# One loop over all turns of a layer's experts, and the overflow part moved behind it

## The chip, the cores and the metric

The kernel runs on one core of a Trainium2 chip. The metric is the device time of one execution in microseconds (us). The kernel before took 1077.97 us, the median of three runs (1076.32, 1077.97 and 1079.43).

## The reference

The program is a two-layer decoder trunk over 256 tokens of width 1024, all in float32. Each layer has a token mixer (a spatial gate with attention in layer 0, a short convolution in layer 1) and then a mixture of 32 experts; the mixture is what the change touches:

```
expert_idx = top_g[:, None] * EXPERTS_PER_GROUP + top_e        # 1 of 4 groups, then 2 of its 8 experts
combine = jnp.sum(one_hot(expert_idx, 32) * weights[..., None], axis=1)
for e in range(N_EXPERTS):                                     # 32
    h = jax.nn.silu(t @ w_gate[e]) * (t @ w_up[e])             # (256,1024) @ (1024,512), twice
    out = out + combine[:, e:e + 1] * (h @ w_down[e])          # (256,512) @ (512,1024)
```

An expert's three matrices are 2 MB each, 6 MB together; two layers of 32 experts read 402 MB of the run's 440 MB.

## The kernel before

The kernel is written engine by engine: each engine has its own program, and semaphores are all that ties them. For each expert up to 32 tokens (CAP) are gathered; a token list longer than that is finished in the overflow part.

For expert e TensorE (PE) does, in this order: gate and up for its 32 gathered tokens (`gate_up`, L1579, 64 float32 matmuls, which the trace shows as 128 matmuls and 128 weight loads of two passes); the scatter of expert e-1's result into the PSUM banks 0 to 3, where the layer's output is summed (`scatter`, L1596); two transposes (L1602); the gather of expert e+1's tokens (L1608); and down (L1588). VectorE (DVE) builds the selection matrices and the product of gate and up; ScalarE (ACT) does silu and copies out of PSUM. SyncE (SP) issues the weight loads into a ring of nine 2 MB slots, that is three experts. Experts 0 to 11 and the last two (30, 31) are loaded matrix by matrix, experts 12 to 29 with one 6 MB transfer each (`whole`, L433), issued once the down of the expert three before has been done (`y_ready`).

The experts are worked on in turns of three (TRI = 3, TURNS = 10, so turns 0 to 9 hold experts 0 to 29). Turn 0 is written out. Then PE has three loops with a body of three experts each: turns 1 to 3 (`apart_expert`, with a wait for each matrix), turn 4 alone (`whole_expert`, one wait), and, after the overflow part, turns 5 to 9 (MIDDLE = 5). SP, ACT and DVE also go through the turns in two loops with the overflow part between them. The last two experts are written out behind the last loop (`last_experts`).

The overflow part stands after expert 14 (PAUSE = MIDDLE*TRI - 1). On PE it begins with `put_x` (L1354), which adds the residual x to the PSUM sums with eight matmuls (16 in the trace). Then each of the four engines reads the number of overflow blocks from memory into a register (`further`, L357) and branches over a body that would scatter the last result and process the blocks, one after the other (`more_experts`, and `overflow` on SP). At 0 blocks the branch is taken and nothing of the body runs.

An engine's instructions come from memory too: the profile's queue q8 carries PE's instruction stream.

Of the kernel before, what the change touches and what calls it, by code (L numbers as in the profile page):

```python
# [23 lines left out]
NE = G * EG  # L24
# [10 lines left out]
RING = 9  # L35
LAG = 2
SLOT = 4096
TRI = 3
# [7 lines left out]
L_EVEN = 0  # L46
EARLY = 2
RING_FIRST = (0, 1, 3)
MIDDLE = 5
PAUSE = MIDDLE * TRI - 1  # L50
SPARE_XG = 1
PER_MOE = 3 * NE - 3
L_MOE = [7, 7 + PER_MOE + 9]
# [13 lines left out]
def entry(l, e):  # L67
    return L_MOE[l] + 3 * (e - (e > EARLY))


def place(n):
    return (n + 2) % RING
# [3 lines left out]
    return place(L_MOE[l] + 3 * i) // 3  # L76


def is_whole(e):
    return FINE <= e < NE - 2  # L80


SINGLE = [z for z in SPLIT if z not in (L_EVEN, L_EVEN + 1, L_ODD)]
for layer in range(2):
    for expert in range(FINE):
        if expert != EARLY:
            SINGLE += [entry(layer, expert) + mat for mat in range(3)]
    SINGLE += [entry(layer, NE - 2) + mat for mat in range(3)]
    SINGLE += [entry(layer, NE - 1) + mat for mat in range(2)]
SINGLE.append(L_GAIN)  # L90
WHOLE = [(layer, expert) for layer in range(2) for expert in range(NE) if is_whole(expert)]


def single_count(n):
    return sum(z <= n and place(z) == place(n) for z in SINGLE)


def whole_count(l, e):
    return sum((zl, ze) <= (l, e) and place(entry(zl, ze)) == place(entry(l, e)) for zl, ze in WHOLE)


def pieces(n):
# [20 lines left out]
def trunk(nc, x_in, even_first, even_second, even_w_in, even_w_out, gmlp_w_s, gmlp_b_s, columns,  # L123
          odd_first, odd_w_in, odd_w_out, norm_gains, router, expert_weights_in, last_down, norm_final, out):
    with ExitStack() as ctx:
# [3 lines left out]
        def sem(name):  # L129
            return ctx.enter_context(nc.semaphore(name))  # L130
# [112 lines left out]


        landed = [sem(f"landed{i}") for i in range(RING)]
        whole_landed = [sem(f"whole_landed{i}") for i in range(RING // 3)]
        gate_used, out_half = sem("gate_used"), sem("out_half")
        first_landed = [sem(f"first_landed{i}") for i in range(len(OPENING))]
        eps_ready = sem("eps_ready")
# [60 lines left out]
        def wide(n):  # L310
            return slot(n).rearrange("p (k f) -> p k f", k=K)

        def tall(n):
            return slot(n).rearrange("p (j d) -> p j d", j=4)
# [33 lines left out]

        def wait_landed(eng, n):

            eng.wait_ge(landed[place(n)], 16 * single_count(n))

        @contextmanager
        def further(eng):
# [24 lines left out]
        def _(sp):  # L379
# [49 lines left out]
            def whole(l, e, i, former):  # L429

                at = third(l, (i - 1) % TRI)
                sp.wait_ge(y_ready, after(l, former))
                sp.dma_start(ring[:, SLOT * 3 * at:SLOT * 3 * (at + 1)], expert_weights_in[l, e]).then_inc(whole_landed[at], 16)  # L433

            def turns(l, start, stop):
                with sp.Fori(start, stop) as b:
                    for i in range(TRI):
                        whole(l, b * TRI + i, i, b * TRI + (i - TRI))
# [16 lines left out]
            def experts(l):  # L455
                if l:
                    first(l, 2, 2)
                    load_spare(l)
                first(l, 0, 0)
                first(l, 0, 1)  # L460
                if l == 0:
                    load_spare(l)
                first(l, 0, 2)
                first(l, 1, 0)
                if l == 0:
                    first(l, 1, 1)
                sp.wait_ge(*((even_lo, 6), (pb_ready, 4))[l])
                load_early(l, 0, 0, 1)
                first(l, 1, 2 - l)
                first(l, 2, 1 - l)  # L470
                load_early(l, 1, 0, 2)
                first(l, 1 + (l == 0), 2 * l)
                first(l, 2, 2 - l)
                load_early(l, 1, 1, 2)
                for e in range(EARLY + 2, FINE):
                    second(l, e)
                for i in range(TRI):
                    e = FINE + i
                    whole(l, e, i, e - TRI)
                turns(l, ROLLED + 1, MIDDLE + 1)  # L480
                overflow(l)
                turns(l, MIDDLE + 1, TURNS)
                for e in LAST_TWO:
                    for mat in range(2):
                        n = entry(l, e) + mat
                        fill(n, matrix(l, e, mat), buffer(n, mat))
                n = entry(l, NE - 2) + 2
                fill(n, matrix(l, NE - 2, 2), tall(n))
                n = entry(l, NE - 1)
                sp.wait_ge(*used_up(n + 2 - RING))  # L490
                for j in range(NP):
                    sp.dma_start(tall(n + 2)[:, j, :], last_down[l, j]).then_inc(quarter_landed[j], 16)
# [76 lines left out]
        def _(act):  # L569
# [197 lines left out]
            def expert(l, e):  # L767
                act.wait_ge(gu_ready, after(l, e))
                act.activation(sg, GU[:, 0:FP], ACT.Silu).then_inc(silu_ready, 1)  # L769
                act.wait_ge(cmb_turned, after(l, e))  # L770
                act.activation(cmb, BB[:, 0:S], ACT.Copy).then_inc(cmb_ready, 1)  # L771
                act.wait_ge(y_ready, after(l, e))
                act.activation(yy, YB[:, 0:DP], ACT.Copy).then_inc(yy_ready, 1)  # L773
# [11 lines left out]
            def moe(l):  # L785

                act.wait_ge(tops_ready, l + 1)
                for t in range(TT):
                    act.activation(gs[:, t, :], lg[:, t, :], ACT.Exp, bias=gneg[:, t:t + 1], scale=rstd[:, t:t + 1],
                                   accum_out=gsum[:, t:t + 1])  # L790
                    last = act.activation(ex[:, t, :], ml[:, t, 0:NE], ACT.Exp, bias=eneg[:, t:t + 1],
                                          scale=rstd[:, t:t + 1])
                last.then_inc(exps_ready, 1)
                preload(ACT.Silu)
                for start, stop in ((0, MIDDLE), (MIDDLE, TURNS)):
                    with act.Fori(start, stop) as b:
                        for i in range(TRI):
                            expert(l, b * TRI + i)
                    if start == 0:
                        more_experts(l)  # L800
                last_experts(l)

            def more_experts(l):
# [42 lines left out]
        def _(dve):  # L846
# [400 lines left out]
            def moe(l):  # L1247

                update(l)
                for t in range(TT):  # L1250
                    copy_turned(l, t)
                invert(l, 1)
                fillers()
                route(l)
                choose(0, count[:, 1:CAP + 1], 0).then_inc(sel_ready, 1)
                gather(l, 0, 0)
                expert_weights(l)
                over_capacity(l)
                weigh(l, 0).then_inc(wsel_ready, 1)
                for i in range(TRI):  # L1260
                    expert(l, 0, i)
                    if i == 0:
                        more_blocks(l)
                for start, stop in ((1, MIDDLE), (MIDDLE, TURNS)):
                    with dve.Fori(start, stop) as b:
                        for i in range(TRI):
                            expert(l, b, i)
                    if start == 1:
                        more_experts(l)
                for e in range(TURNS * TRI, NE):  # L1270
                    expert(l, e // TRI, e % TRI, last=e == NE - 1)

# [53 lines left out]
        def _(pe):  # L1326
# [328 lines left out]

                expert(l, EARLY, EARLY, wait_weights, lambda mat: lambda k: halves[mat][k // HK][:, k % HK, :], spare)

            def apart_expert(l, T, i):
                n = entry(l, TRI + i)

                def wait_weights(mat):
                    pe.wait_ge(landed[place(n + mat)], (T + (single_count(n + mat) - 1)) * 16)

                expert(l, T * TRI + i, i, wait_weights, lambda mat: lambda k: wide(n + mat)[:, k, :], tall(n + 2))

            def whole_expert(l, T, i):
                n = entry(l, FINE + i)

                def wait_weights(mat):
                    if mat == 0:  # L1670
                        pe.wait_ge(whole_landed[place(n) // 3], (T + (whole_count(l, FINE + i) - ROLLED)) * 16)

                expert(l, T * TRI + i, i, wait_weights, lambda mat: lambda k: wide(n + mat)[:, k, :], tall(n + 2))

# [15 lines left out]
            def moe(l):  # L1690
# [26 lines left out]
                for e in range(TRI):  # L1717
                    if e == EARLY:
                        early_expert(l)
                    else:  # L1720
                        first_expert(l, e)
                with pe.Fori(1, ROLLED) as T:
                    for i in range(TRI):
                        apart_expert(l, T, i)
                with pe.Fori(ROLLED, MIDDLE) as T:
                    for i in range(TRI):
                        whole_expert(l, T, i)
                for t in range(TT):
                    put_x(t)
                more_experts(l)  # L1730
                with pe.Fori(MIDDLE, TURNS) as T:
                    for i in range(TRI):
                        whole_expert(l, T, i)
                last_experts(l)
                scatter_result(l, NE - 1).then_inc(o_ready, 1)

# [83 lines left out]
```

## Time and profile before

| what | value |
|---|---|
| median of three runs | 1077.97 us |
| span of the profiled execution | 1076.0 us |
| PE busy, weight loads busy | 820.6 us (76%), 653.4 us (61%) |
| DVE, ACT, POOL busy | 315.3, 192.6, 5.4 us |
| memory traffic | 439.94 MB, mean 409 GB/s |
| instructions on PE | 13956 matmuls, 13957 weight loads |

The profile was taken from one execution. Its own time is its span, 1076.0 us; it is 1.97 us below the median of the three runs. A wait named `<-DMA` is one for weights. `<-issue` is time in which an engine waited for nothing that the profile shows. Layer 0's experts run from about 113 to 537 us of the span, the odd layer's mixer from 542 to 634 us, and layer 1's experts from 643 to 1067 us. Expert 12 of layer 0 begins its gate at 255.54 us, expert 15 behind the overflow part at 302.92 us, expert 29 at 505.42 us and expert 30 at 514.40 us; in layer 1 the same experts begin at 786.10, 832.26, 1035.31 and 1045.56 us.

### The profile page before, as it was taken

What the parts mean: (1) busy time and instruction counts of PE and PEld (TensorE: products, weight loads), DVE (VectorE), ACT (ScalarE), POOL (GpSimd) and SP (SyncE); (2) the same over time, 40 slices, a digit from 0 to 9 for tenths busy, and PEclk for the clock granted to TensorE, in tenths of its full rate; (3) what the DMA queues carried; (4) which work ended last, traced back from release to release, by engine and by line L of the source; (5) the groups of instructions that cost most, each with busy time, mean ns of one, the idle gap of its engine ahead of it and who ended that gap; (6) DMA issues with size and microseconds to landing.
All of it is one profiled execution on the core that took longest, in us unless ns stands there. A gap on an engine that the chain in (4) does not pass through costs nothing.

```text
span 1076.0 us, 30244 instructions
## 1 busy us (share of the span) xinstructions
PE 820.6 (76%) x13956; PEld 653.4 (61%) x13957; DVE 315.3 (29%) x782; ACT 192.6 (18%) x360; POOL 5.4 (1%) x26
## 2 busy tenths in 40 slices
PE   9999989673767667666899999896556767666685
PEld 9778757452654545555599977664354545555463
DVE  5764522211111111111277744221101111111112
ACT  6764211000000000000254331010000000000002
POOL 1000000000000000000000000000000000000000
PEclk9999999987887888888999999998879888888889
DMA  9987999999999999999998599999999999999995
GB/s 375 427 332 282 422 427 427 429 441 425 433 427 434 433 432 431 433 433 421 418 428 336 219 396 424 426 427 429 444 425 428 432 432 433 429 435 433 433 420 242
DMA packets 24948, 439.94 MB, mean 409 GB/s; under 512 B 2992, under 2 KB 3504, under 8 KB 8240
## 3 DMA queue, kind: packets, MB, share of 16 engines
q1 hardware_dynamic: 23904, 437.58, 95.9%
q10 hardware_dynamic: 976, 1.33, 0.4%
q8 instruction: 58, 0.95, 0.4%
q14 instruction: 10, 0.08, 0.0%
HBM read 437.84 MB, written 1.05 MB: 408 GB/s over the span
## 4 chain that ended last, share of the span: by engine, by line
DMA 53%; PE 40%; issue 4%; DVE 2%; SPq 1%; ACT 1%; DVEq 0%; ACTq 0%
DMA ring<-in_expert_weights 50%; PE psum L1579 12%; PE psum L1375 6%; PE psum L1588 6%; PE psum L1448 4%; PE psum L1596 3%; PE psum L1608 3%; PE psum L1427 2%; DMA ring<-in_even_w_in 2%; DMA m<-in_gmlp_w_s 1%; PE psum L1602 1%; PE psum L1700 1%; DVE ring_halves L875 0%; PE psum L1347 0%; PE psum L1334 0%
## 5 line engine op out<-in xcount | busy, mean ns | idle before, releaser
L1579 PE MATMUL psum<-ring,m 128*32 128x128 f32 x7936 | 304.1, 322 | 221.5 <-DMA ring<-in_expert_weights 187.2
L1579 PEld LDWEIGHTS psum<-ring,m 128*32 128x32 f32 x7936 | 280.7, 132 | 252.5 <-issue 177.9
L1236 DVE TENSOR_TENSOR m<-psum,m 128x128 f32<-128x128 f32 x64 | 18.7, 292 | 549.3 <-ACT m L769 532.4
L1588 PE MATMUL psum<-ring,m 128*32 128x256 f32 x1984 | 123.3, 387 | 5.2 <-DMA ring<-in_expert_weights 3.9
L769 ACT ACTIVATE m<-psum 128x128 f32<-128x128 f32 x60 | 16.7, 278 | 497.1 <-PE psum L1579 497.1
L1375 PE MATMUL psum<-scr_halves,ring_halves 128*128 128x256 f32 x736 | 99.1, 284 | 0.2 <-ACT ring_halves L603 0.2
L1588 PEld LDWEIGHTS psum<-ring,m 128*32 128x32 f32 x1984 | 66.1, 113 | 52.9 <-issue 12.1
L1375 PEld LDWEIGHTS psum<-scr_halves,ring_halves 128*128 128x128 f32 x736 | 94.3, 193 | 0.5 <-ACT ring_halves L603 0.5
L1596 PE MATMUL psum<-m 32*128 32x256 f32 x1024 | 81.1, 420 | 10.6 <-issue 8.5
L1608 PE MATMUL psum<-x,m 128*32 128x256 f32 x1024 | 72.7, 402 | 1.4 <-issue 0.8
L1596 PEld LDWEIGHTS psum<-m 32*128 32x128 f32 x1024 | 50.2, 195 | 29.6 <-issue 23.6
L875 DVE TENSOR_TENSOR ring_halves<-ring,ring_halves 128x2048 fp32r<-128x2048 f32 (+1 forms) x32 | 63.6, 2021 | 12.4 <-ACT ring_halves L603 12.4
L603 ACT ACTIVATE ring_halves<-ring 128x2048 fp32r<-128x2048 f32 (+2 forms) x40 | 57.8, 1477 | 31.7 <-PE psum L1375 24.4
L1210 DVE STREAM_TRANSPOSE m<-psum 128x256 f32<-128x256 f32 x64 | 28.8, 450 | 105.4 <-PE psum L1608 105.4
L773 ACT ACTIVATE m<-psum 128x256 f32<-128x256 f32 x60 | 23.0, 384 | 157.7 <-PE psum L1588 157.7
L1608 PEld LDWEIGHTS psum<-x,m 128*32 128x32 f32 x1024 | 27.6, 112 | 25.0 <-issue 13.8
L1219 DVE TENSOR_SCALAR m<-count,pos,cw 128x128 f32<-128x128 f32 x128 | 38.2, 341 | 0.1
L771 ACT ACTIVATE m<-psum 128x256 f32<-128x256 f32 x60 | 23.0, 384 | 83.5 <-PE psum L1602 83.4
L1448 PE MATMUL psum<-ring_halves,aux_halves 128*128 128x512 f32 x96 | 33.2, 400 | 0.0
L1205 DVE TENSOR_SCALAR m<-count,pos,rstd 128x32 f32<-128x32 f32 x128 | 32.1, 294 | 2.1 <-issue 1.8
L1602 PE MATMUL psum<-ident,m 128*128 128x128 f32 x128 | 28.8, 307 | 0.0
L1213 DVE TENSOR_TENSOR m<-m,gains 128x256 f32<-128x256 f32 x64 | 27.2, 425 | 2.2
(196 smaller groups left out, 522.5 us busy)
## 6 DMA issues: line engine op xcount, KB each, us to landing
ring<-in_expert_weights SPq DMA_DIRECT2D x36, 6144.0 KB, 33.7
ring<-in_expert_weights SPq DMA_DIRECT2D x76, 2048.0 KB, 21.9
ring<-in_odd_w_in SPq DMA_DIRECT2D x5, 2048.0 KB, 26.0
ring<-in_even_w_in SPq DMA_DIRECT2D x3, 2048.0 KB, 22.2
ring<-in_even_w_out SPq DMA_DIRECT2D x2, 2048.0 KB, 31.4
spare<-in_expert_weights SPq DMA_DIRECT2D x2, 2048.0 KB, 24.7
ring<-in_last_down SPq DMA_DIRECT2D x8, 512.0 KB, 32.1
ring<-in_odd_w_out SPq DMA_DIRECT2D x2, 2048.0 KB, 28.9
```

The source lines that it names most:

```text
L603: act.activation(hi_slot(n)[:, c], raw_part(n, part), ACT.Copy).then_inc(w_hi, 1)
L875: dve.tensor_tensor(lo_slot(n)[:, c], raw_part(n, part), hi_slot(n)[:, c].bitcast(F32), ALU.subtract).then_inc(w_lo, 1)
L1205: last = dve.tensor_scalar(sel[:, t, CAP * i:CAP * (i + 1)], ranks, pos[:, bass.ds(at(e, t), 1)], rstd[:, t:t + 1], ALU.is_equal, ALU.mult)
L1210: return dve.transpose(xg[:, i, :, :], XB[:, 0:DP].rearrange("p (q k) -> p k q", k=K))
L1219: last = dve.tensor_scalar(wsel[:, t, :].rearrange("p (n c) -> p n c", n=NP), count[:, 1:CAP + 1].unsqueeze(1).to_broadcast([P, NP, CAP]), ...
L1375: return pe.matmul(bank[banks[c // 2]][:, (c % 2) * S:(c % 2 + 1) * S], w[a][:, k, P * c:P * (c + 1)], h[b][:, k, :], start=k == 0 and a + ...
L1448: last = pe.matmul(bank[2 * t + c][:, :], mix[a][:, 4 * r + j, P * t:P * (t + 1)], w[b][:, j, 512 * c:512 * (c + 1)], start=r == 0 and j = ...
L1579: last = pe.matmul(GU[CAP * part:CAP * (part + 1), lo:lo + FP], block_of(k), w_of(k)[:, FP * part:FP * (part + 1)], start=k == 0, stop=k = ...
L1588: last = pe.matmul(YB[CAP * part:CAP * (part + 1), 0:DP], h[:, CAP * f:CAP * (f + 1)], w[:, f, DP * part:DP * (part + 1)], start=f == 0, s ...
L1596: last = pe.matmul(bank[part][:, DP * t:DP * (t + 1)], cmb[r, P * t:P * (t + 1)], yy[r, :], start=first and t == 0, stop=False, skip_group ...
L1602: last = pe.transpose(BB[:, P * t:P * (t + 1)], wsel[:, t, :], ident[:, :])
L1608: last = pe.matmul(XB[CAP * part:CAP * (part + 1), 0:DP], sel[:, t, CAP * i:CAP * (i + 1)], x[:, t, DP * part:DP * (part + 1)], start=t == ...
```

## The change

PE, ACT and DVE go through all turns of a layer in one loop; SP has one loop for the loads of experts 15 to 29. The overflow part with `put_x` stands behind the loop, that is after expert 29 and before the last two (PAUSE = 29). On PE the bodies of turn 4 and of turns 5 to 9 are gone, since one body now serves turns 1 to 9. To make that possible all experts count on the same semaphores: a whole 6 MB load increments the first slot's semaphore when it lands, and SP increments the other two right after it has issued the load, so that the body's waits for matrices 1 and 2 are met. A whole expert so has two more waits on PE than before.

```diff
-MIDDLE = 5
-PAUSE = MIDDLE * TRI - 1
+PAUSE = TURNS * TRI - 1
...
-                sp.dma_start(ring[:, SLOT * 3 * at:SLOT * 3 * (at + 1)], expert_weights_in[l, e]).then_inc(whole_landed[at], 16)
+                sp.dma_start(ring[:, SLOT * 3 * at:SLOT * 3 * (at + 1)], expert_weights_in[l, e]).then_inc(landed[3 * at], 16)
+
+                sp.sem_inc(landed[3 * at + 1], 16)
+                sp.sem_inc(landed[3 * at + 2], 16)
...
-                turns(l, ROLLED + 1, MIDDLE + 1)
+                turns(l, ROLLED + 1, TURNS)
                 overflow(l)
-                turns(l, MIDDLE + 1, TURNS)
...
-                for start, stop in ((0, MIDDLE), (MIDDLE, TURNS)):
-                    with act.Fori(start, stop) as b:
-                        for i in range(TRI):
-                            expert(l, b * TRI + i)
-                    if start == 0:
-                        more_experts(l)
+                with act.Fori(0, TURNS) as b:
+                    for i in range(TRI):
+                        expert(l, b * TRI + i)
+                more_experts(l)
                 last_experts(l)
...
-            def whole_expert(l, T, i):
-                n = entry(l, FINE + i)
+            def later_expert(l, T, i):
+                n = entry(l, TRI + i)
 
                 def wait_weights(mat):
-                    if mat == 0:
-                        pe.wait_ge(whole_landed[place(n) // 3], (T + (whole_count(l, FINE + i) - ROLLED)) * 16)
+                    pe.wait_ge(landed[place(n + mat)], (T + (landed_count(n + mat) - 1)) * 16)
...
-                with pe.Fori(1, ROLLED) as T:
+                with pe.Fori(1, TURNS) as T:
                     for i in range(TRI):
-                        apart_expert(l, T, i)
-                with pe.Fori(ROLLED, MIDDLE) as T:
-                    for i in range(TRI):
-                        whole_expert(l, T, i)
+                        later_expert(l, T, i)
                 for t in range(TT):
                     put_x(t)
                 more_experts(l)
-                with pe.Fori(MIDDLE, TURNS) as T:
-                    for i in range(TRI):
-                        whole_expert(l, T, i)
                 last_experts(l)
```

On PE, the program before has these rows in layer 1 where the loop of turn 4 ends (L1588 is the down of expert 14) and the overflow part begins (L1354 is `put_x`, L357 the load of the count, L370 the branch over the body).

```order
L1588 MATMUL psum<-ring,m 32x256 x16
L1725 REGISTER_ALU
L1725 COMPARE_AND_BRANCH
L1354 MATMUL psum<-x,ident 128x256 x8
L357 TENSOR_LOAD extra
L357 ISA x2
L370 COMPARE_AND_BRANCH
L1596 MATMUL psum<-m 128x256 x8
```

And these are the rows where the branch arrives, behind the overflow body: the loop of turns 5 to 9 (L1731), whose first expert is 15.

```order
L1757 REGISTER_ALU
L370 UNCONDITIONAL_BRANCH
L1731 UNCONDITIONAL_BRANCH
L1731 ISA
L1671 ISA
L1579 MATMUL psum<-ring,m 32x128 x64
```

In the changed kernel the same part follows the only loop (L1698, turns 1 to 9; L1573 is now the down of expert 29, L1339 is `put_x`, L344 the load of the count and L357 the branch).

```order
L1573 MATMUL psum<-ring,m 32x256 x16
L1698 REGISTER_ALU
L1698 COMPARE_AND_BRANCH
L1339 MATMUL psum<-x,ident 128x256 x8
L344 TENSOR_LOAD extra
L344 ISA x2
L357 COMPARE_AND_BRANCH
L1581 MATMUL psum<-m 128x256 x8
```

Here the branch arrives at the last two experts of layer 1: gate and up of 30, scatter, transposes, gather, gate and up of 31 (all L1564), nine filling matmuls (L1345), down of 30, scatter, transposes, down of 31, scatter.

```order
L357 UNCONDITIONAL_BRANCH
L1564 MATMUL psum<-ring,m 32x128 x64
L1581 MATMUL psum<-m 128x256 x8
L1587 MATMUL psum<-ident,m 128x128 x2
L1593 MATMUL psum<-x,m 32x256 x8
L1564 MATMUL psum<-ring,m 32x128 x64
L1345 MATMUL psum<-nones 128x128 x9
L1573 MATMUL psum<-ring,m 32x256 x16
L1581 MATMUL psum<-m 128x256 x8
L1587 MATMUL psum<-ident,m 128x128 x2
L1573 MATMUL psum<-ring,m 32x256 x16
L1581 MATMUL psum<-m 128x256 x8
```

So `put_x` and the jump have moved from before expert 15 to before expert 30, and the code that runs for the first time behind the jump is no longer that of a loop but that of the last two experts.

## Rows read from the trace of the kernel before

**Rows 1.** The page: the chain that ended last, shares by engine.

```profile
DMA 53%; PE 40%; issue 4%; DVE 2%; SPq 1%; ACT 1%; DVEq 0%; ACTq 0%
```

**Rows 2.** Stretch of layer 0's turns 6 to 9: busy, PEclk, DMA share, GB/s.

```profile
345.00:505.30 160.30, 107.36 (x2134) 84.05 (x2134) 27.52 (x88) 11.50 (x33) 0.00 (x0) 0.85 1.00 431
```

**Rows 3.** Chain in time: start us, us, what; experts 12, 19, 22, then layer 1's 12, 19.

```profile
255.54 5.34 PE psum L1579 x128
...
360.09 5.37 PE psum L1579 x128
...
403.69 6.34 PE psum L1579 x128
...
786.10 6.28 PE psum L1579 x128
...
889.96 5.57 PE psum L1579 x128
```

**Rows 4.** Instruction queue: packets, MB, share; whole run, 240:345, 345:515, 515:545 us.

```profile
q8 instruction: 58, 0.95, 0.4%
...
q8 instruction: 11, 0.18, 0.7%
...
q8 instruction: 1, 0.02, 0.0%
...
q8 instruction: 3, 0.05, 0.7%
```

**Rows 5.** PE timeline at the pause of layer 0.

```profile
295.35 3.72 PE L1354 MATMUL psum<-x,ident 128*128 128x256 f32 x16
302.92 3.46 PE L1579 MATMUL psum<-ring,m 128*32 128x128 f32 x65 [3.85 <-issue]
309.96 3.49 PE L1579 MATMUL psum<-ring,m 128*32 128x128 f32 x63 [3.57 <-issue]
```

**Rows 6.** PE timeline at the pause of layer 1.

```profile
824.34 3.72 PE L1354 MATMUL psum<-x,ident 128*128 128x256 f32 x16
832.26 0.52 PE L1579 MATMUL psum<-ring,m 128*32 128x128 f32 x3 [4.20 <-issue]
839.17 5.36 PE L1579 MATMUL psum<-ring,m 128*32 128x128 f32 x125 [6.39 <-issue]
...
846.01 1.14 PE L1596 MATMUL psum<-m 32*128 32x256 f32 x14 [0.85 <-issue]
```

**Rows 7.** Timeline of layer 1's last three experts, PE, and SP's loads for them.

```profile
1009.53 17.12 SPq L381 DMA_DIRECT2D ring<-in_expert_weights  x5
...
1035.31 6.27 PE L1579 MATMUL psum<-ring,m 128*32 128x128 f32 x128 [5.34 <-DMA ring<-in_expert_weights]
...
1045.56 3.68 PE L1579 MATMUL psum<-ring,m 128*32 128x128 f32 x128
...
1052.76 1.96 PE L1579 MATMUL psum<-ring,m 128*32 128x128 f32 x64 [1.08 <-issue]
...
1054.94 1.95 PE L1579 MATMUL psum<-ring,m 128*32 128x128 f32 x64 [0.23 <-DMA ring<-in_expert_weights]
...
1059.89 1.93 PE L1588 MATMUL psum<-ring,m 128*32 128x256 f32 x32 [0.79 <-DMA ring<-in_expert_weights]
...
1066.25 1.15 PE L1596 MATMUL psum<-m 32*128 32x256 f32 x16 [0.55 <-DVE m L1241]
```

**Rows 8.** PE timeline of layer 0's last two experts.

```profile
514.40 3.68 PE L1579 MATMUL psum<-ring,m 128*32 128x128 f32 x128
...
529.85 1.93 PE L1588 MATMUL psum<-ring,m 128*32 128x256 f32 x32 [0.79 <-DMA ring<-in_expert_weights]
...
536.21 1.15 PE L1596 MATMUL psum<-m 32*128 32x256 f32 x16 [0.55 <-DVE m L1241]
```

**Rows 9.** Chain in time, the odd layer's projections.

```profile
554.38 57.59 PE psum L1375 x480
```

**Rows 10.** The page: products of gate and up, one for each expert.

```profile
L1236 DVE TENSOR_TENSOR m<-psum,m 128x128 f32<-128x128 f32 x64 | 18.7, 292 | 549.3 <-ACT m L769 532.4
```

More of the change, by code:

```diff
@@ L76, in third, with landed_count @@
     return place(L_MOE[l] + 3 * i) // 3
-def is_whole(e):
-    return FINE <= e < NE - 2
-SINGLE = [z for z in SPLIT if z not in (L_EVEN, L_EVEN + 1, L_ODD)]
+COUNTED = [z for z in SPLIT if z not in (L_EVEN, L_EVEN + 1, L_ODD)]
 for layer in range(2):
-    for expert in range(FINE):
+    for expert in range(NE):
         if expert != EARLY:
[L87 to L99, printed above, removed]
+            COUNTED += [entry(layer, expert) + mat for mat in range(3 - (expert == NE - 1))]
+COUNTED.append(L_GAIN)
+def landed_count(n):
+    return sum(z <= n and place(z) == place(n) for z in COUNTED)
 def pieces(n):
@@ L245, in trunk @@
         landed = [sem(f"landed{i}") for i in range(RING)]
-        whole_landed = [sem(f"whole_landed{i}") for i in range(RING // 3)]
         gate_used, out_half = sem("gate_used"), sem("out_half")
@@ L349, in wait_landed @@
         def wait_landed(eng, n):
-            eng.wait_ge(landed[place(n)], 16 * single_count(n))
+            eng.wait_ge(landed[place(n)], 16 * landed_count(n))
         @contextmanager
@@ L1263, in moe @@
                         more_blocks(l)
-                for start, stop in ((1, MIDDLE), (MIDDLE, TURNS)):
-                    with dve.Fori(start, stop) as b:
-                        for i in range(TRI):
-                            expert(l, b, i)
-                    if start == 1:
-                        more_experts(l)
+                with dve.Fori(1, TURNS) as b:
+                    for i in range(TRI):
+                        expert(l, b, i)
+                more_experts(l)
                 for e in range(TURNS * TRI, NE):
@@ L1656, in early_expert @@
                 expert(l, EARLY, EARLY, wait_weights, lambda mat: lambda k: halves[mat][k // HK][:, k % HK, :], spare)
-            def apart_expert(l, T, i):
+            def later_expert(l, T, i):
                 n = entry(l, TRI + i)
                 def wait_weights(mat):
-                    pe.wait_ge(landed[place(n + mat)], (T + (single_count(n + mat) - 1)) * 16)
-                expert(l, T * TRI + i, i, wait_weights, lambda mat: lambda k: wide(n + mat)[:, k, :], tall(n + 2))
-            def whole_expert(l, T, i):
-                n = entry(l, FINE + i)
-                def wait_weights(mat):
-                    if mat == 0:
-                        pe.wait_ge(whole_landed[place(n) // 3], (T + (whole_count(l, FINE + i) - ROLLED)) * 16)
+                    pe.wait_ge(landed[place(n + mat)], (T + (landed_count(n + mat) - 1)) * 16)
                 expert(l, T * TRI + i, i, wait_weights, lambda mat: lambda k: wide(n + mat)[:, k, :], tall(n + 2))
@@ L1730, in moe @@
                 more_experts(l)
-                with pe.Fori(MIDDLE, TURNS) as T:
-                    for i in range(TRI):
-                        whole_expert(l, T, i)
                 last_experts(l)
```

## The prediction

> **What bounds the kernel now.** I read the chain that ended last first, by engine and then in order of time. It lies on DMA for 53% and on PE for 40% of the span, with 4% "issue" [rows 1]. The DMA share is that of the experts: in layer 0's turns 6 to 9 the DMA engines are busy at 1.00 and PE for 107.36 of 160.3 us [rows 2]. PE's experts then start as their 6 MB land: experts 19 to 22 take 403.69 - 360.09 = 43.60 us, 14.53 us each [rows 3]. PE needs some 10 us for an expert, so a delay of a few us in the middle of a layer is made good by the next experts. Two places have no such cover. One is the end of layer 1: in the timeline, expert 30 starts at 1045.56, right behind expert 29's down without a wait; expert 31's up waits 0.23 us for weights and expert 30's down 0.79 us; the last scatter ends at 1066.25 + 1.15 = 1067.40 [rows 7]. PE's slack against DMA there is 0.23 + 0.79 = 1.0 us. The other is the end of layer 0: the same 1.0 us or a little more [rows 8], and then the odd layer, in which PE's products run 57.59 us in one piece [rows 9], so that PE passes every delay on, and with it the release of ring slots for layer 1's loads. What ends a layer late ends the run late.
>
> The second view is the instruction queue and the "issue" waits. No overflow block runs: the product of gate and up runs 64 times, 2 x 32 experts [rows 10]. So in both kernels PE only jumps over that body. Of the 58 packets of PE's instructions (0.95 MB, 16 KB each) 11 move from 240 to 345 us, where the bodies of turn 4 and turn 5 and the jump stand, and one from 345 to 515 us, where the same body repeats [rows 4]: loops run from code that is on the engine, new code is fetched. At the jump PE stands still: in layer 0 `put_x` begins at 295.35 and the next expert at 302.92, 7.57 us later; in layer 1 at 824.34 and 832.26, 7.92 us [rows 5, 6]. Then it stops again: 302.92 to 309.96 (7.04 us), 832.26 to 839.17 (6.91), 839.17 to 846.01 (6.84), the last after 127 matmuls with as many weight loads, which is one packet of 256 instructions. Warm, 128 matmuls take 3.68 us (expert 30, [rows 7]). So code that runs for the first time while weights stream comes at about half of PE's pace.
>
> **The parts of the change.** (a) Two loop bodies less on PE, in each layer. PE's stops there cost nothing directly, since the weights land later; what they cost is DMA time. Experts 12 to 19 of layer 0 take 360.09 - 255.54 = 104.55 us, where seven at 14.53 us take 101.7; in layer 1 889.96 - 786.10 = 103.86 [rows 3]. The surplus, 2.8 and 2.1 us, falls where 11 instruction packets each go through the same DMA engines. I take all of it as won: -4.9 us. Bounds: 0 (it has another cause) and -4.9.
>
> (b) The waits on PE. Two more per whole expert stand beside a wait for weights of about 5 us (5.34 before expert 29, [rows 7]): 0. SP's two increments follow an issue that nobody waits for: 0. On SP the overflow part stands between expert 29's load and the five loads for the last two, which now begin at 1009.53 [rows 7] for data that PE wants from 1045.56. A jump of PE's price, 7.9 us, on SP would leave those on time: 0, and if this cover were gone the price would be up to 7.9 us in each layer. ACT and DVE also jump; their next product for the last experts is wanted only after PE's own jump: 0.
>
> (c) The pause before expert 30, layer 1. `put_x` and the jump: expert 30's gate starts not at 1045.56 but 7.7 us later (mean of 7.57 and 7.92), at 1053.3. All that follows is new code: counted in the order (four instructions to a float32 matmul, two to a transpose), from gate of 30 to the last scatter are 812 instructions, 3.2 packets. In the kernel before one packet of it was already there, since PE comes to it from the loop in sequence and expert 30 shows no stop. Counted from where the stops fell in rows 5 and 6, the first packet's edge stands some 200 instructions behind the jump's target in layer 1, and some 25 in layer 0. For a packet I take 6.0 us: rows 5 and 6 have 6.84 to 7.04 under the full stream; the floor is no stop at all, 3.68; at the end of a layer the loads are smaller and run out, so I go a little below the rows. Then: start 1053.3; edge after 100 matmuls, code there at 1059.3; gate and up done 1060.2; expert 31's gate 3.5 us later as before (1052.76 - 1049.24), 1063.7; next edge already met, done 1067.6; from there to the last scatter's end 1067.40 - 1056.89 - 0.79 = 9.7 us as before: 1077.3. A stopped PE also comes back slower: expert 12's gate and up took 5.34 us after a wait, against 3.68 [rows 3, 7], and the granted clock of turns 6 to 9 is 0.85 of full speed, a mix of its levels of 1.2 and 2.4 GHz [rows 2]. I add 0.6 for it. End at 1077.9: +10.5 us.
>
> (d) The same in layer 0. `put_x` at 514.40, target reached at 522.1, edge after 12 matmuls, so code at 528.1; gate and up done 531.5; next edge at 534.1 in the middle of scatter and gather; expert 31's gate at 536.3; edge at 540.1; done 540.8; plus 9.7 gives 550.5, plus 0.6 for the clock 551.1, against 536.21 + 1.15 = 537.36: +13.7. If the target's packet is there already when the loop ends (it is the packet next to the loop's last one), the jump costs only `put_x`, 3.72 us, and the sum falls to +8. I take +12. The bounds for (c) and (d) are each 2.7 (below) and 18.
>
> Sum on the profiled execution's own time: 1076.0 - 4.9 + 10.5 + 12 = 1093.6. It stood 2.0 us below the median of the runs, so the prediction is 1095.6, rounded to 1095.
>
> The Trainium skill bears on this twice, both in "Runtime: NRT & Kernel Launch", section "Instruction fetch mechanics". It says that code comes in 16 KiB blocks of 256 instructions, and that crossing into the next block is "mostly hidden"; the size agrees with this trace, the hiding does not, where 6.84 us pass for a block whose work takes 3.68. By that rule only the jump would cost, which is the first rival below. It also says that prefetch is purely sequential and that nothing is gained from locality; by that a body of three experts would be fetched anew in all nine turns. The trace has one packet in four turns, so this doesn't weigh.
>
> **The rivals.** *Only the jump costs.* Packets behind it arrive in time, because at a layer's end the stream thins out. Each layer then pays 7.7 - 1.0 = 6.7 us: 1076.0 - 4.9 + 13.4 + 2.0 = 1086.5. For it: in the kernel before three packets come in 515 to 545 us [rows 4] and no stop shows. Against it: those were asked for while PE had work, and in layer 0 the first edge is only 25 instructions away.
>
> *The code is there: not slower.* If PE holds the packets behind the loop, since the loop runs nine turns in which nothing else is fetched, the jump has nothing to wait for and only `put_x` stands in the way: 3.7 - 1.0 = 2.7 us per layer, against the 4.9 us of (a): 1076.0 + 5.4 - 4.9 + 2.0 = 1078.5, no change; with a part of `put_x` beside the wait for expert 31's weights, 1076. It decides below about 3.5 us per layer. Against it: both jumps of the trace stalled [rows 5, 6], and layer 1's target lies two packets on.
>
> *Everything is missed.* Packets at 7.0 us, the jump at 7.9, the lower clock throughout, and the next packet not asked for before the jump: 13 us in layer 1 and 18 in layer 0, less 4.9: 1104.
>
> *The body doesn't stay loaded.* Nine turns of fetching would take DMA time at (a)'s rate, 4.9/22 = 0.22 us a packet, five packets in eight more turns of two layers: 18 us on top of the forecast, 1113. One packet in four turns speaks against it.
>
> **The numbers.** Forecast (stops behind both jumps) 0.62; only the jump 0.17; code is there 0.11; everything missed 0.08; the body refetched 0.02. The range, 1084 to 1103, leaves out the third, most of the last two and the ends of the unknown packet time. What this measurement can tell from no change is 0.3%, 3.2 us. Of the third rival half lies within that and half below; adding a little for a gain in (a) larger than shown: faster 0.05, same 0.06, slower 0.89.
>
> **What would show it.** PE's timeline behind `put_x` of layer 1 should show the gate of 30 starting 7 to 8 us after `put_x`, and one "issue" stop of 2 us or more inside gate and up; in layer 0 such a stop within the first 12 to 20 matmuls. Expert 29 should begin about 2.8 us earlier in layer 0, and the instruction queue should move some 40 packets instead of 58, none or one between turns 2 and 9. The odd layer's 57.6 us should be as long as before but 8 to 10 us later. I am wrong if PE goes from `put_x` to expert 30 within 4 us, if the last weights land later than before by more than layer 0's delay, or if SP's loads of the last two experts start late.

## The result and the profile after

The changed kernel took 1093.16 us (median of five runs, 1090.96 to 1095.77) against 1076.32 us of the kernel before on the same chip (also five runs; 1077.97 above is the median of three of them): the ratio is 1.0156, 95% interval 1.0142 to 1.017, so it is 16.8 us slower. The prediction was 1095, the range 1084 to 1103. The span of the profiled execution is 1091.4 us, 15.4 more than before.

The page of the changed kernel, the chain by engine and PE's instruction queue, which answer to [rows 1] and to the first of [rows 4] (58 packets):

```profile
DMA 53%; PE 41%; issue 3%; DVE 2%; SPq 1%; ACT 1%; DVEq 0%; ACTq 0%
...
q8 instruction: 40, 0.66, 0.2%
```

The shares hardly differ, which is why they can't tell where 15.4 us went. The 18 packets that are gone are the two bodies in each layer. In the window 240 to 500 us the queue q8 has no packet at all. What counts is the two ends of layers. (An edge, below, is the place in the code where one packet of 256 instructions ends and the next begins.) PE's timeline at the end of layer 0, which answers to [rows 8]; L1564 is gate and up, L1339 `put_x`, L1581 the scatter, L1573 down, L1345 the nine filling matmuls:

```profile
502.17 6.13 PE L1564 MATMUL psum<-ring,m 128*32 128x128 f32 x128 [5.46 <-DMA ring<-in_expert_weights]
...
512.40 3.72 PE L1339 MATMUL psum<-x,ident 128*128 128x256 f32 x16
516.05 0.63 PE L1564 MATMUL psum<-ring,m 128*32 128x128 f32 x12
519.55 5.14 PE L1564 MATMUL psum<-ring,m 128*32 128x128 f32 x116 [2.87 <-issue]
524.62 1.77 PE L1581 MATMUL psum<-m 32*128 32x256 f32 x16
...
528.84 3.11 PE L1564 MATMUL psum<-ring,m 128*32 128x128 f32 x105 [1.08 <-issue]
534.94 1.51 PE L1564 MATMUL psum<-ring,m 128*32 128x128 f32 x23 [3.00 <-issue]
536.37 3.00 PE L1345 MATMUL psum<-nones 128*128 128x128 f32 x18
...
545.67 1.15 PE L1581 MATMUL psum<-m 32*128 32x256 f32 x16 [0.55 <-DVE m L1228]
```

Expert 30 starts right behind `put_x`, runs 12 matmuls and stops; it stops again 23 matmuls before the end of expert 31's gate and up. (The 1.08 us at 528.84 is no stop for code: the kernel before has the same idle time there [rows 7]. The profile names no releaser; In layer 1 of the kernel before DVE's product for the gathered tokens ends at 1052.65 and PE goes on at 1052.76, so I read it as a wait for DVE.) The last scatter ends at 546.82, 9.46 us later than before, though expert 29 had started 3.25 us sooner.

The end of layer 1, which answers to [rows 7]:

```profile
1042.95 5.37 PE L1564 MATMUL psum<-ring,m 128*32 128x128 f32 x128 [5.09 <-DMA ring<-in_expert_weights]
...
1052.41 3.72 PE L1339 MATMUL psum<-x,ident 128*128 128x256 f32 x16
1059.47 4.71 PE L1564 MATMUL psum<-ring,m 128*32 128x128 f32 x102 [3.33 <-issue]
1064.86 1.06 PE L1564 MATMUL psum<-ring,m 128*32 128x128 f32 x26 [0.68 <-issue]
...
1069.44 3.70 PE L1564 MATMUL psum<-ring,m 128*32 128x128 f32 x128 [1.08 <-issue]
...
1075.27 1.94 PE L1573 MATMUL psum<-ring,m 128*32 128x256 f32 x32
...
1081.64 1.15 PE L1581 MATMUL psum<-m 32*128 32x256 f32 x16 [0.55 <-DVE m L1228]
```

Here the jump itself stops PE: expert 30 starts 7.06 us after `put_x` began. One short stop follows after 102 matmuls, and no wait for weights is left: the 0.23 and 0.79 us of slack in [rows 7] are used up. The last scatter ends at 1082.79, 15.39 us later than before.

The same stretches by engine, from `put_x` (in the kernel before, from expert 30) to the last scatter. The columns are busy time and count of PE, weight loads, DVE, ACT and POOL, then the granted clock, the DMA share and GB/s. First the changed kernel, then the kernel before:

```profile
512.40:546.80 34.40, 26.41 (x426) 20.14 (x422) 3.71 (x11) 4.52 (x9) 0.00 (x0) 0.90 1.02 422
1052.40:1082.80 30.40, 24.24 (x426) 18.63 (x422) 3.71 (x11) 3.57 (x8) 0.00 (x0) 0.94 0.61 250
```

```profile
514.40:537.40 23.00, 18.70 (x410) 13.75 (x402) 3.58 (x11) 4.63 (x9) 0.00 (x0) 1.00 1.01 416
1045.60:1067.40 21.80, 18.66 (x410) 13.72 (x402) 3.54 (x11) 3.58 (x8) 0.00 (x0) 1.00 0.78 321
```

16 matmuls more take 7.7 and 5.6 us more of PE's busy time, of which `put_x` is 3.7: PE runs the rest slower, at a granted clock of 0.90 and 0.94 instead of 1.00. Layer 1's end is cheaper than layer 0's, and its DMA share is 0.61 where layer 0's is 1.02, with the odd layer's weights in the stream.

Measured from expert to expert, the 15.4 us are: up to expert 12 of layer 0, -0.5; experts 12 to 29 of layer 0, -2.8; from expert 29 to the first expert of layer 1, +12.6; to its expert 12, +0.3; experts 12 to 29, -2.0; from expert 29 to the end, +7.8.

The ends hold more than the pause. In layer 0's end the +12.6 are `put_x` 3.65, the two stops 5.87, slower matmuls 4.0, and 1.2 for expert 29's own gate and up (6.13 us against 5.00), less 2.1 of waits for weights that are used up. In layer 1's end the +7.8 are 7.06 up to the arrival of the jump, 0.68 for the stop and 1.9 for slower matmuls, less 0.8, since expert 29's gate and up happened to be faster (5.37 us against 6.27), and less 1.0 of used-up waits.

### The profile page after: what moved, and what is told of

The parts are those of the page before. It is cut to its first block, busy times and chain, and to the rows that moved or that the text cites. A ratio compares the mean times of both kernels' runs of the same rounds, so it can differ in the third digit from the quotient of the medians.

```text
span 1091.4 us, 30380 instructions
## 1 busy us (share of the span) xinstructions
PE 824.9 (76%) x13956; PEld 661.4 (61%) x13957; DVE 315.2 (29%) x782; ACT 192.3 (18%) x360; POOL 5.4 (0%) x26
## 4 chain that ended last, share of the span: by engine, by line
DMA 53%; PE 41%; issue 3%; DVE 2%; SPq 1%; ACT 1%; DVEq 0%; ACTq 0%
DMA ring<-in_expert_weights 50%; PE psum L1564 13%; PE psum L1360 6%; PE psum L1573 5%; PE psum L1433 4%; PE psum L1581 3%; PE psum L1593 3%; PE psum L1412 2%; DMA ring<-in_even_w_in 2%; DMA m<-in_gmlp_w_s 1%; PE psum L1587 1%; PE psum L1345 1%; PE psum L1339 1%; PE psum L1676 1%; DVE ring_halves L862 0%
## 5 line engine op out<-in xcount | busy, mean ns | idle before, releaser
L1564 PE MATMUL psum<-ring,m 128*32 128x128 f32 x7936 | 316.0, 332 | 237.7 <-DMA ring<-in_expert_weights 220.4
L1564 PEld LDWEIGHTS psum<-ring,m 128*32 128x32 f32 x7936 | 292.3, 136 | 270.8 <-DMA ring<-in_expert_weights 133.8
L1573 PE MATMUL psum<-ring,m 128*32 128x256 f32 x1984 | 119.7, 380 | 2.5 <-DMA ring<-in_expert_weights 1.4
L1573 PEld LDWEIGHTS psum<-ring,m 128*32 128x32 f32 x1984 | 64.6, 110 | 48.2 <-issue 7.5
L1581 PE MATMUL psum<-m 32*128 32x256 f32 x1024 | 76.8, 406 | 6.4 <-issue 4.3
L1581 PEld LDWEIGHTS psum<-m 32*128 32x128 f32 x1024 | 48.1, 188 | 23.5 <-issue 17.9
## 6 DMA issues: line engine op xcount, KB each, us to landing
ring<-in_odd_w_out SPq DMA_DIRECT2D x2, 2048.0 KB, 16.8
```

Of the source, the lines that this page charges most:

```text
L1564: last = pe.matmul(GU[CAP * part:CAP * (part + 1), lo:lo + FP], block_of(k), w_of(k)[:, FP * part:FP * (part + 1)], start=k == 0, stop=k = ...
L1573: last = pe.matmul(YB[CAP * part:CAP * (part + 1), 0:DP], h[:, CAP * f:CAP * (f + 1)], w[:, f, DP * part:DP * (part + 1)], start=f == 0, s ...
L1581: last = pe.matmul(bank[part][:, DP * t:DP * (t + 1)], cmb[r, P * t:P * (t + 1)], yy[r, :], start=first and t == 0, stop=False, skip_group ...
```

## Experiments

The table has all runs beside the two kernels. "12 to 29" is the time from the start of expert 12's gate to that of expert 29, "end 0" from there to layer 1's first expert, "end 1" from expert 29 of layer 1 to the end of the span. The ratio is to the kernel before on the same chip, whose median was 1076.41 us beside the first four and 1076.86 us beside the last four. The four stretches come from one profiled execution each, whose time lies between 1.5 us below (putx_early) and 2.8 us above (dead64) the median of its kernel; it is 2.2 to 2.5 us above for no_jump, move_only and merge_only, and 1.7 for neither. A difference of 1 to 2 us in one end is therefore no finding by itself; "12 to 29" is steadier, 247.1 or 247.2 us in both layers of six of the rows below.

| kernel | median us | ratio, 95% interval | q8 packets | 12 to 29, layer 0 / 1 | end 0 | end 1 |
|---|---|---|---|---|---|---|
| before | 1076.32 | | 58 | 249.9 / 249.2 | 140.1 | 40.7 |
| changed | 1093.16 | 1.0156 (1.0142 to 1.017) | 40 | 247.1 / 247.2 | 152.7 | 48.5 |
| no_jump | 1078.17 | 1.0016 (1.0007 to 1.0026) | 36 | 247.2 / 247.1 | 141.1 | 46.7 |
| putx_early | 1091.91 | 1.0156 (1.0136 to 1.0175) | 40 | 247.2 / 247.2 | 151.3 | 47.8 |
| dead64 | 1098.39 | 1.0204 (1.0187 to 1.0221) | 41 | 247.2 / 247.2 | 159.9 | 48.7 |
| move_only | 1094.19 | 1.0164 (1.0147 to 1.0181) | 49 | 248.1 / 247.4 | 151.0 | 51.8 |
| merge_only | 1076.00 | 0.9987 (0.9979 to 0.9996) | 49 | 247.2 / 248.5 | 142.4 | 41.7 |
| three_loops | 1095.61 | 1.0183 (1.0169 to 1.0196) | 58 | 249.0 / 249.1 | 147.0 | 52.9 |
| pause_first | 1087.20 | 1.009 (1.0072 to 1.0107) | 40 | 247.2 / 247.2 | 144.3 | 40.5 |
| neither | 1073.97 | 0.9974 (0.9965 to 0.9984) | 36 | 247.2 / 247.1 | 141.5 | 41.0 |

### The two halves of the change: move_only and merge_only

The first is the kernel before with the pause moved and the bodies left apart:

```diff
-PAUSE = MIDDLE * TRI - 1
+PAUSE = TURNS * TRI - 1
...
-                with pe.Fori(ROLLED, MIDDLE) as T:
+                with pe.Fori(ROLLED, TURNS) as T:
                     for i in range(TRI):
                         whole_expert(l, T, i)
                 for t in range(TT):
                     put_x(t)
                 more_experts(l)
-                with pe.Fori(MIDDLE, TURNS) as T:
-                    for i in range(TRI):
-                        whole_expert(l, T, i)
```

> The kernel before with nothing changed but the place of the overflow part and put_x, now behind turn 9; the bodies for turns 1 to 3 and for whole experts stay apart, with their own semaphores. Theory (the move is the loss): layer 0's target is two packets on with half a packet left behind it, layer 1's two with 0.6 left; ends longer by 11 and 8.5 us, and half of the 5 us of the fewer packets is won: 1092 to 1095 us. Rival (merging the bodies is a part of the loss): under 1088 us.

It took 1094.19 us, within the theory's range and far from the rival's. Its ends are 10.9 and 11.1 us longer than before: layer 0's as expected, layer 1's 2.6 us more, with a stop of 2.28 us at an edge after 76 matmuls. The second is the changed kernel with the pause back behind turn 4:

```diff
-                with pe.Fori(1, TURNS) as T:
+                with pe.Fori(1, MIDDLE) as T:
                     for i in range(TRI):
                         later_expert(l, T, i)
                 for t in range(TT):
                     put_x(t)
                 more_experts(l)
+                with pe.Fori(MIDDLE, TURNS) as T:
+                    for i in range(TRI):
+                        later_expert(l, T, i)
```

> The changed kernel with the overflow part and put_x back behind turn 4: the merged body stands twice on PE (turns 1 to 4 and 5 to 9), all experts count on the same semaphores. Theory (merging alone wins the DMA time of some nine packets, its waits cost nothing): about half of the 5 us: 1073 to 1075 us against 1076.3 before. Rival (two more waits per expert cost PE time): 1076 us or more.

It took 1076.00 us, 0.13% under the kernel before: outside the theory's 1073 to 1075 us and on the edge of the rival's range. So the move is the whole loss, and merging costs nothing. Against the rival speak experts 12 to 29, where the added waits stand, with 2.7 and 0.7 us less than before. The expected gain of about 2.5 us came only in part, since layer 0's end is 2.3 us longer. There expert 31's up waits for its weights, 4.03 us where the kernel before waits 1.34 us (first line merge_only, second line before; L1570 is gate and up in merge_only):

```profile
525.18 2.98 PE L1570 MATMUL psum<-ring,m 128*32 128x128 f32 x64 [4.03 <-DMA ring<-in_expert_weights]
...
524.90 1.95 PE L1579 MATMUL psum<-ring,m 128*32 128x128 f32 x64 [1.34 <-DMA ring<-in_expert_weights]
```

PE came 1.4 us sooner to expert 29, but these weights landed no sooner, so the lead was lost here. Why they didn't, and how much of it belongs to this one execution, stays open. Of all kernels run that do the whole work this one is the fastest, and the only one that beats both, though by less than 0.2%.

### What the pause costs: no_jump, putx_early and neither

```diff
-                more_experts(l)
                 last_experts(l)
```

(on PE, ACT and DVE, and `overflow(l)` on SP)

> The changed kernel without the overflow part (no engine reads the count or jumps; its code is left out, and with it what it would do for a token list over 32, of which there is none here); put_x stays where it is. Theory (what the pause costs at a layer's end is the jump to code that is not there, and the stops behind it): PE goes from put_x into expert 30 without a stop, each layer's end costs only put_x, 3.7 us less 1.0 us of slack, and the time falls from 1093 to 1076 to 1079 us. Rival (the merged loop with its waits, or SP's order, is what costs): stays at 1090 or more.

It took 1078.17 us, 15 us less than the changed kernel and within the theory's range: the jump and what follows from it are nearly all of the loss. PE's timeline of no_jump (L1336 is `put_x`, L1561 gate and up, L1342 the filling matmuls), first layer 0, then layer 1:

```profile
512.85 3.72 PE L1336 MATMUL psum<-x,ident 128*128 128x256 f32 x16
516.50 3.70 PE L1561 MATMUL psum<-ring,m 128*32 128x128 f32 x128
...
523.73 3.70 PE L1561 MATMUL psum<-ring,m 128*32 128x128 f32 x128 [1.08 <-issue]
...
1045.40 3.70 PE L1561 MATMUL psum<-ring,m 128*32 128x128 f32 x128
...
1059.03 3.07 PE L1342 MATMUL psum<-nones 128*128 128x128 f32 x17 [2.20 <-issue]
```

Expert 30 follows `put_x` at once, and all 128 matmuls of gate and up run in one piece. The expectation said "without a stop", and at this place it holds; but one edge falls into the filling matmuls of layer 1 and costs 2.20 us there, so that end 1 is only 1.8 us shorter than in the changed kernel. Nearly all that this kernel wins it wins in layer 0 (11.6 us). The two profiled executions differ by 12.7 us, a little less than the medians (15.0), since no_jump's is the slowest of its ten runs.

```diff
+                for t in range(TT):
+                    put_x(t)
                 with pe.Fori(1, TURNS) as T:
                     for i in range(TRI):
                         later_expert(l, T, i)
-                for t in range(TT):
-                    put_x(t)
                 more_experts(l)
```

> The changed kernel with put_x ahead of the loop (behind turn 0), the overflow part still behind the loop. Theory (the wait for code is what PE is stopped by, and put_x runs inside it): only the 0.9 us by which the jump is reached sooner is won in each layer: 1090 to 1092 us. Rival (put_x is 3.7 us of work on the path of each layer): 1093.2 - 7.4 = 1086 us.

It took 1091.91 us, as the theory said, at a ratio that can't be told from the changed kernel's. Its timeline in layer 0 and, from the third line, in layer 1:

```profile
511.19 0.63 PE L1564 MATMUL psum<-ring,m 128*32 128x128 f32 x12 [0.17 <-issue]
516.86 6.07 PE L1564 MATMUL psum<-ring,m 128*32 128x128 f32 x116 [5.04 <-issue]
...
1056.32 5.56 PE L1564 MATMUL psum<-ring,m 128*32 128x128 f32 x102 [5.85 <-issue]
```

The 12 matmuls are there again, and the stops are 5.04 and 5.85 us where they were 2.87 and 3.33: each took up what `put_x` left, less 1.2 to 1.5 us, and the matmuls behind it ran slower (6.07 us against 5.14, 5.56 against 4.71). Of 7.4 us of work taken out beside the waits for code at most 1.3 us were won. With both edits together nothing stands between loop and expert 30:

```diff
+                for t in range(TT):
+                    put_x(t)
                 with pe.Fori(1, TURNS) as T:
                     for i in range(TRI):
                         later_expert(l, T, i)
-                for t in range(TT):
-                    put_x(t)
-                more_experts(l)
                 last_experts(l)
```

> The changed kernel without the overflow part (as above: what it would do for a list over 32 is left out) and with put_x ahead of the loop: nothing stands between the loop and expert 30. Theory: the floor of this form, 1070 to 1072 us; against the version with put_x alone at the end it wins what put_x costs there when no jump covers it, 2.7 us or a little more per layer. Rival (put_x at the end is hidden beside the wait for weights): the same as that version.

It took 1073.97 us, 4.2 us less than no_jump. That is above the theory's 1070 to 1072. So putting `put_x` early is worth 4.2 us over both layers where no jump covers it; where one does, the two ends are 1.4 and 0.7 us shorter. But the theory's 2.7 us per layer did not come. In end 0 there is no difference (141.5 against 141.1), because expert 31's up now waits for its weights, and in layer 0 the rival holds:

```profile
524.01 3.43 PE L1561 MATMUL psum<-ring,m 128*32 128x128 f32 x64 [2.42 <-DMA ring<-in_expert_weights]
```

By the profiles all of it lies in end 1 (46.7 against 41.0). About 4.0 us of these 5.7 fall before expert 30's gate, where `put_x` was; the rest is the stop in the filling matmuls, 1.17 us instead of 2.20, and faster matmuls around it. (Like no_jump, this version leaves the overflow part out.)

### Where the code lies: dead64

```diff
                         pe.wait_ge(X["evac"], n)
+                        keep_busy(64, BB)
```

> The changed kernel with 64 more float32 matmuls, 256 instructions, in the overflow body, which never runs: all code behind moves by exactly one packet. Theory (layer 0's jump was free because its target lay in the packet next to the loop's last one, layer 1's target was already two away): layer 0's jump now stops PE for 3 to 4 us and the first edge still comes 12 matmuls later, so layer 0's end is 5 to 7 us longer, layer 1's the same: 1098 to 1100 us. Rival (the distance of a jump does not matter, code that never runs costs nothing): 1093 us.

1098.39 us, as the theory said: 256 instructions that never run cost 5.2 us. Layer 0's end in its trace:

```profile
513.10 3.72 PE L1339 MATMUL psum<-x,ident 128*128 128x256 f32 x16
520.48 0.63 PE L1564 MATMUL psum<-ring,m 128*32 128x128 f32 x12 [3.66 <-issue]
526.42 4.00 PE L1564 MATMUL psum<-ring,m 128*32 128x128 f32 x69 [5.30 <-issue]
```

The jump now stops PE (3.66 us where there was no stop), 12 matmuls follow as before, and then the next packet is awaited for 5.30 us instead of 2.87. End 0 is 7.2 us longer, end 1 0.2 us, in an execution 2.8 us above the median. This shows two things at once: the jump over one packet fewer was free in the changed kernel, and the edge is where the count of instructions puts it. It also tells the jump from the reading of the count ahead of it: both kernels read it at the same place, and only the distance of the target changed.

### What a packet costs the stream: three_loops

```diff
-                with pe.Fori(1, TURNS) as T:
-                    for i in range(TRI):
-                        later_expert(l, T, i)
+                for start in (1, 4, 7):
+                    with pe.Fori(start, start + 3) as T:
+                        for i in range(TRI):
+                            later_expert(l, T, i)
```

> The changed kernel with its loop over turns 1 to 9 written as three loops of three turns with the same body: 9 more packets of code per layer in the middle of the stream, no other instruction. Theory (a packet costs about 0.2 us of DMA time): expert 29 starts 3 to 4 us later than in the changed kernel in layer 0, and 2 more in layer 1; at the layers' ends the edges fall otherwise (layer 0's jump target two packets on with 0.87 left: about 3 us less), so the time is 1092 to 1097 us, and the start of expert 29 in layer 0 is what tells. Rival (the gain of the changed kernel before expert 29 has another cause, such as PE coming to the down earlier): expert 29 of layer 0 starts within 0.5 us of the changed kernel's.

Experts 12 to 29 take 249.0 and 249.1 us instead of 247.1 and 247.2. By the number that I had named, expert 29's start in layer 0, it is less clear: 504.38 against 502.17 us, 2.2 us later, where 3 to 4 were expected and under 0.5 by the rival. 18 packets of code in the stream cost 3.8 us, 0.21 us each on average. The same matmuls, waits and loads run, only from new code, and the delay in layer 0 falls where new code comes: with the third loop, which begins at expert 21, experts 22 and 23 take 15.2 and 15.3 us where 14.4 to 14.6 is the rule. The DMA share from expert 12 to 29 stays at 1.00 in both kernels, so the stream was not starved by PE's stops. What else a packet does to the stream the runs don't show. The time, 1095.61 us, lies within the expectation, but not for its reasons alone: end 0 is 5.7 us shorter and end 1 4.4 us longer than in the changed kernel, as the edges fall otherwise.

### The pause where the stream should cover it: pause_first

```diff
+                for t in range(TT):
+                    put_x(t)
+                more_experts(l)
                 with pe.Fori(1, TURNS) as T:
                     for i in range(TRI):
                         later_expert(l, T, i)
-                for t in range(TT):
-                    put_x(t)
-                more_experts(l)
```

> The changed kernel with the overflow part and put_x ahead of the one loop, behind turn 0 (PAUSE = 2): one body, few packets, and the jump at a place where the ring's loads are 15 to 20 us ahead of PE. Theory: both layers keep the won DMA time, 5 us, and neither pays at its end: 1070 to 1073 us, faster than both kernels. Rival (PE is the bound in the first turns, where it stops for its own code): the jump's 7 us appear in each layer, 1083 us or more.

1087.20 us: my theory fell, and the time lies in the rival's range. PE's timeline of pause_first (L1344 is `put_x`, L1569 expert 3's gate and up), and its stretch from 140 to 160 us:

```profile
143.58 3.72 PE L1344 MATMUL psum<-x,ident 128*128 128x256 f32 x16
151.13 6.57 PE L1569 MATMUL psum<-ring,m 128*32 128x128 f32 x128 [3.83 <-issue]
```

```profile
140.00:160.00 20.00, 16.17 (x218) 11.90 (x214) 2.59 (x8) 1.04 (x3) 0.00 (x0) 0.74 0.63 246
```

The same stretch of the kernel before:

```profile
140.00:160.00 20.00, 17.49 (x388) 12.58 (x384) 5.00 (x16) 2.09 (x6) 0.00 (x0) 0.93 1.01 427
```

The ring is full when the experts begin, so a PE that stops releases no slot and the stream dries up: DMA share 0.63 instead of 1.01. SP jumps here too, but it isn't what holds the loads up. Its waits from 120 to 175 us are all for PE, here as in the kernel before. The lines show the larger group of each, first pause_first's (total, times, longest); the longest wait, 23.8 us, ends with the load that goes out at 154.83 us, when PE is 3.7 us into expert 3's gate and up:

```profile
SPq L369 <- PE psum L1569: 34.5, 7, 23.8
...
SPq L381 <- PE psum L1579: 28.4, 8, 13.6
```

Expert 12 starts 261.4 us into the span instead of 255.0 in the changed kernel; in layer 1 the same stretch is 3.3 us longer than there, not the rival's 7. One more part of the loss stands in neither account: layer 0's end, without jump or `put_x` in it, is still 4.3 us longer than in the kernel before, because two edges behind the loop stop PE for 0.90 and 3.27 us. I had read the long time from issue to landing as a reserve, and it is none while the ring is full and PE, slowed by its own new code, sets the pace.

## Why the prediction was right

The time, the sign and the mechanism came out. By its steps:

(a) Fewer bodies: -4.9 us taken; measured from expert 12 to 29, -2.8 and -2.0, that is -4.8. three_loops puts two bodies per layer back and so accounts for 3.8 of it. The rest may belong to the pause, which left the same stretch in the same change; no run separates the two. The price is not even, either: merge_only has one body more than the changed kernel, and the pause, and pays 0.1 us for both in layer 0 and 1.3 in layer 1.

(b) Waits, SP, ACT and DVE at 0: right. merge_only has the added waits and increments and isn't slower than before. The jumps of ACT and DVE at their new place show no wait on PE: behind them it waits 0.50 and 0.55 us for the two engines, as before. SP's five loads for the last two experts began at 476.69 and 1017.50 us, 25 us ahead of expert 29.

(c) Layer 1's end: +10.5 taken, +7.8 measured. The jump was nearly as sized (7.06 us from `put_x` against 7.7), and the stop behind it was too dear: the packet after the jump came 1064.86 - 1059.47 = 5.4 us later, not 6.0, and the slower clock hid part of it, since 102 matmuls took 4.71 us instead of the 2.9 that I had counted. The stop was 0.68 us, not 3. The stream was thinner there (DMA share 0.61) than I allowed for. Another 0.8 us is luck: expert 29's gate and up was that much faster than in the kernel before.

(d) Layer 0's end: +12 taken, as a value between +13.7 (the jump stalls) and +8 (the target's packet is there); +12.6 measured. The sum hits for a mixed reason, and in part by luck. The jump did not stall, which was the case that I had priced at +8. By its own working that price is too low: `put_x` alone, 3.7 us instead of 7.7, takes 4.0 off 13.7 and leaves +9.7. The stops were 2.87 and 3.00 us. The edge in the middle of the scatter cost 0.34 us at most; PE passed it at 525.69 and the packet behind it was there only at 534.94, more than 9 us later, where I had taken 6.0. At a granted clock of 0.90 the matmuls took about 4 us more than at 1.00; I had put 0.6 us for the clock. And the slack was not the 1.0 us or a little more that I had read: expert 31's up had waited 1.34 us for weights (the line at 524.90 above) and expert 30's down 0.79, together 2.1 us. Had the jump stalled, the end would have been dead64's, +19.8.

The odd layer passed the delay on: its projections ran 57.59 us as before and began at 563.76 instead of 554.38 us.

The rivals: *only the jump costs* (1086.5) falls with the stops in both timelines, though in layer 1 it is nearly right. *The code is there* (1078.5) is right about layer 0's jump and wrong in its price, since the packet behind it wasn't there. *The body doesn't stay loaded* is excluded by the empty instruction queue from 240 to 500 us; so by the rule of the Trainium skill ("Runtime: NRT & Kernel Launch", section "Instruction fetch mechanics") that prefetch is purely sequential without any gain from locality, these nine turns should have fetched, and they did not. The same section gives TensorE an instruction memory of 128 KiB, and that fits the trace: a body is 18/4 = 4.5 packets of 16 KB, 72 KB. What that section says of jumps, that a taken branch out of the loaded window stops the engine for a fetch, agrees: 7.06 us in layer 1, and dead64's 3.66 us stop for a target moved by one packet.

## What to carry to other kernels

A delay costs little as long as a stream ahead of it makes it good; so a jump, a pause or code that runs for the first time belongs in the middle of a memory-bound stretch, not at its end (merge_only against the changed kernel: 17 us) and not where the buffers are full and the engine sets the pace (pause_first: 10 us over the kernel before, with 9.5 us more ahead of the two experts 12). Count the instructions between a jump and its target and behind it: on this chip code that never runs moved the time by 5.2 us. And work that stands beside a fetch of code is nearly free, so taking it out wins little before the fetch is gone (putx_early: at most 1.3 us for 7.4 us of work).

## What the hardware showed that I had not expected

A stop for code comes with a second price, the clock: it stood at 0.90 and 0.94 of full speed over the two ends, where it was 1.00 before, so that 116 matmuls took 5.14 us instead of 3.3, in layer 0 about 4 us in all. And instruction packets of 16 KB, 0.2 to 0.4% of the DMA engines' time, slow a saturated weight stream by about 0.21 us each on average, while their share of the engines' time, 0.4% of 1076 us for 58 packets [rows 4], is 0.07 us each; why they cost three times that, and why unevenly, no run here tells.
